# Issuing the odd conditioning-weight transfers of the prelude from GpSimd's queue

## What is computed

```python
cond = silu(c)
for i in range(2):
    mod = einsum('bd,sdk->bsk', cond, ada_w[i]) + ada_b[i]      # ada_w: (2 layers, 2 sub-layers, 2048, 3*2048)
    h = modulate(rmsnorm(x, norm_g[i, 0]), shift_t, scale_t)
    y = pool_mixer(h, ...) if i == 0 else retention(h, ...)
    x = x + gate_t * y
    h = modulate(rmsnorm(x, norm_g[i, 1]), shift_m, scale_m)
    x = x + gate_m * (relu(h @ w1[i]) ** 2 @ w2[i])
return rmsnorm(x, final_g)
```

## Time and profile before

| what | value |
|---|---|
| time, median of 3 runs | 2337.06 us (2336.86 to 2339.1) |
| span of the profiled execution | 2336.1 us |
| own time of the profiled execution | not listed apart from its span |
| TensorE matmul busy | 2251.9 us, 96% |
| VectorE busy | 1681.1 us, 72% |
| ScalarE busy | 1084.2 us, 46% |
| GpSimd busy | 139.9 us, 6% |
| moved by DMA | 664.21 MB, mean 284 GB/s |
| chain that ended last | PE 88%, of it line 701 86% |

### The profile page before, as it was taken

How to read it: one execution, slowest core, us unless ns; L and a number is a source line. 1 busy time by engine, 2 the same in 40 slices (tenths; PEclk the granted TensorE clock), 3 DMA queues, 4 the chain that set the end, 5 groups by cost and what they waited for, 6 DMA issues and landing times.

```text
span 2336.1 us, 28515 instructions
## 1 busy us (share of the span) xinstructions
PE 2251.9 (96%) x10033; PEld 1817.7 (78%) x10033; DVE 1681.1 (72%) x1814; ACT 1084.2 (46%) x1342; POOL 139.9 (6%) x249
## 2 busy tenths in 40 slices
PE   4489999999999999999999999999999999999998
PEld 2147788888888887888888888887888888888887
DVE  4668889788887898777676767677877555555557
ACT  2324554544544545444454444555553453453454
POOL 0000000100100100001000001000100000000000
PEclk9689999999999999999999999999999999999999
DMA  9999989998998977888766887876997776776774
GB/s 400 415 413 393 339 297 328 364 367 277 368 334 292 362 281 231 303 264 275 246 233 215 299 260 244 273 239 202 333 359 248 235 230 195 226 232 191 232 228 152
DMA packets 276674, 664.21 MB, mean 284 GB/s; under 512 B 21768, under 2 KB 22200, under 8 KB 269632
## 3 DMA queue, kind: packets, MB, share of 16 engines
q1 hardware_dynamic: 260320, 611.92, 75.8%
q0 software_dynamic: 15328, 49.87, 6.2%
q10 hardware_dynamic: 896, 0.75, 0.1%
HBM read 638.30 MB, written 24.14 MB: 284 GB/s over the span
## 4 chain that ended last, share of the span: by engine, by line
PE 88%; DMA 2%; DVE 2%; ACT 1%; issue 0%; POOLq 0%; POOL 0%; SPq 0%; DVEq 0%; ACTq 0%
PE acc L701 86%; DMA raw<-in_mlp_w 2%; PE acc L1122 1%; DVE w_lo L1601 1%; PE score_ps L1109 0%; ACT w_hi L1173 0%; DVE ada_acc L1607 0%; PE score_ps L908 0%; PE tb L848 0%; DVE ev L1903 0%; PE tb L983 0%; DVE x L1907 0%; DVE scratch L1773 0%; DVE scratch L1768 0%; PE mod_ps L856 0%
## 5 line engine op out<-in xcount | busy, mean ns | idle before, releaser
L1601 DVE TENSOR_TENSOR w_lo<-raw,w_hi 128x1024 fp32r<-128x1024 f32 x775 | 943.3, 1223 | 558.6 <-ACT w_hi L1173 555.5
L1173 ACT ACTIVATE w_hi<-raw 128x1024 fp32r<-128x1024 f32 x775 | 821.8, 1061 | 1094.8 <-PE acc L701 971.5
L701 PE MATMUL acc<-w_hi,h_lo 128*128 128x512 f32 x1788 | 698.5, 391 | 2.6 <-issue 1.6
L701 PE MATMUL acc<-w_hi,h_hi 128*128 128x512 f32 x1788 | 695.8, 389 | 0.0
L701 PE MATMUL acc<-w_lo,h_hi 128*128 128x512 f32 x1788 | 695.8, 389 | 0.0
L701 PE MATMUL acc<-w_hi,a_lo 128*128 128x512 f32 x1308 | 511.6, 391 | 0.4 <-DVE w_lo L1601 0.4
L701 PE MATMUL acc<-w_lo,a_hi 128*128 128x512 f32 x1308 | 510.3, 390 | 0.0
L701 PE MATMUL acc<-w_hi,a_hi 128*128 128x512 f32 x1308 | 510.0, 390 | 0.0
L701 PEld LDWEIGHTS acc<-w_hi,h_lo 128*128 128x128 f32 x1788 | 335.7, 188 | 75.1 <-issue 4.1
L701 PEld LDWEIGHTS acc<-w_hi,h_hi 128*128 128x128 f32 x1788 | 335.7, 188 | 70.0
L701 PEld LDWEIGHTS acc<-w_lo,h_hi 128*128 128x128 f32 x1788 | 335.8, 188 | 68.5
(11 more groups left out here) (216 smaller groups left out, 912.9 us busy)
## 6 DMA issues: line engine op xcount, KB each, us to landing
raw<-in_mlp_w SPq DMA_DIRECT2D x512, 512.0 KB, 5.1
ada_raw<-in_ada_w SPq DMA_DIRECT2D x248, 512.0 KB, 6.6
raw<-in_ret_w_in SPq DMA_DIRECT2D x192, 512.0 KB, 4.6
ada_early_h<-in_ada_w SPq DMA_DIRECT2D x32, 1024.0 KB, 13.4
raw<-in_ret_w_out SPq DMA_DIRECT2D x64, 512.0 KB, 4.4
ada_raw<-in_ada_w SPq DMA_DIRECT2D x16, 1024.0 KB, 12.5
square_blocks<-ev POOLq DMA_DIRECT2D x112, 128.0 KB, 4.8
ev<-square_blocks POOLq DMA_DIRECT2D x28, 512.0 KB, 6.4
```

Of the source, the lines that this page charges most:

```text
L701: mm = nc.tensor.matmul(acc[pair][t][:], l[:, CK * c + j, tok], w[:, slot, j, :], start=first and j == 0 and i == 0, stop=last and j == CK ...
L1173: nc.scalar.activation(w_hi[:, o % RING], raw[:, o % RING], ACT.Copy).then_inc(hi_ready, 1)
L1601: nc.vector.tensor_tensor(w_lo[:, o % RING], raw[:, o % RING], w_hi[:, o % RING].bitcast(F32), ALU.subtract).then_inc(lo_ready, 1)
```

## The change

The even pieces w0, w2, ... w14 of the three wide segments stay on SP, the odd ones are issued by GpSimd. SP's `load_early` now returns for every slot that isn't a multiple of 4. GpSimd gets `load_odd`, with the same wait for the place's earlier contents. Since a segment's odd pieces are TensorE's and 12 slots hold three of them, GpSimd waits on `ada_pe` alone and SP, in these segments, on `ada_done` alone. The odd pieces signal three new semaphores, `odd_in`, and both readers wait on `wide_in(slot)`. `unsignalled` corrects the counts of segments 3 and 4. GpSimd issues w1 to w9 of segment 0, then the first reciprocal root, then all other odd pieces, then the second root. Places, number and sizes of the transfers stay.

```diff
+        odd_in = [sem(f"odd_wide_piece_in{i}") for i in range(EARLY // 4)]
...
+        def wide_in(slot):
+
+            return odd_in[slot // 4] if slot % 4 else ada_in[slot]
+
         def unsignalled(slot):
 
-            return WIDE_SEGS * SEG // EARLY if slot % 2 else 0
+            return WIDE_SEGS * SEG // EARLY if slot % 4 else 0
...
-                if wide and a % 2:
+                if wide and a % 4:
                     return
...
-                        pe.wait_ge(ada_in[slot], early_loads(seg, a))
+                        pe.wait_ge(wide_in(slot), early_loads(seg, a))
...
-                        dve.wait_ge(ada_in[slot - half], early_loads(seg, a - half))
+                        dve.wait_ge(wide_in(slot - half), early_loads(seg, a - half))
...
+            ada_rows = ada_w.rearrange("i s d (j k) -> (i s) d j k", j=3)
+
+            def load_odd(seg, w):
+
+                g = seg * SEG + 2 * w
+                if g >= EARLY:
+                    if ON_PE[g - EARLY]:
+                        pool.wait_ge(ada_pe, PE_BEFORE[g - EARLY + 1] + 1)
+                    else:
+                        pool.wait_ge(ada_done, DVE_BEFORE[g - EARLY + 1] + 1)
+                slot, to = wide_slot(seg, 2 * w)
+                pool.dma_start(to, ada_rows[0, w * P:(w + 1) * P, seg, :]).then_inc(odd_in[slot // 4], 16)
...
-            for _ in range(2):
-                inverse_root()
+            for w in range(1, 11, 2):
+                load_odd(0, w)
+            inverse_root()
+            for w in range(11, KT, 2):
+                load_odd(0, w)
+            for seg in range(1, WIDE_SEGS):
+                for w in range(1, KT, 2):
+                    load_odd(seg, w)
+            inverse_root()
```

## The result

| | before | after |
|---|---|---|
| median, 12 runs each | 2337.47 us | 2342.59 us |
| lowest to highest | 2336.53 to 2340.18 | 2338.51 to 2345.79 |
| ratio after / before | | 1.0019, interval 1.0011 to 1.0027 |
| span of the profiled execution | 2336.1 us | 2340.1 us |

The ratio is 4.4 us of 2337.5, with an interval from 2.6 to 6.3; the two medians lie 5.1 us apart, which is within it. So the change makes the kernel slightly slower, by about the 0.2% that I had taken for what a measurement can tell. With 12 runs it can be told. Forecast were +3.5 us and 2340.5.

What follows compares the result with a forecast made beforehand. The prediction took the prelude to be bound by DMA transfers of fixed bytes, with TensorE's unchanged stretch after it. Terms 2.48 + 1.0 gave +3.5 us, a forecast of 2340.5 us, range 2334.5 to 2347.5.

Steps and rivals of the forecast that it cites:

- the end of segment 2: Segment 2's last pieces: with queues treated equally, w14 lands last, one piece later; +2.48 us, bounds 0 and 2.48.
- the tail: End of segment 2: after GpSimd issues w15, SP alone feeds the engines with three places; +1.0 us, from 0 to 2.9.
- segments 0 and 1: Ends of these segments: w14 lands with w15, 2.5 us later, but queued transfers cover it; cost 0.
- DMA-bound prelude, fixed bytes: Prelude: DMA engines always busy from 2 to 175 us, bytes unchanged, so DMA time fixed except for rate and empty queues.
- Issue time: Wide pieces: GpSimd gains 24 issues of about 0.58 us, SP loses 24 of 0.33; covered by queued pieces, cost 0.
- Start and root gate: Kernel start: x up to 5 us later, within slack; w11 waits for the first root, bounds 0 and 2.5; both 0.
- The dip: 175 to 185 us, at 359 GB/s: 1.2 us to be won; bounds -1.2 and 0, taken as 0.
- The rate: Wide segments, 119 us of 48 pieces: time per byte alike for both queues; bounds -2.8 and +4.2 us, taken as 0.
- Rival A: Wide pieces: transfers from GpSimd's queue are slower under load; +7.7 us, 2344.8, chance 0.15.
- Rival B: Segment 2's end and 28 to 33 us: DMA engines run dry, on the slower side; +7.9, 2345 us, chance 0.13.
- C: Wide segments: queues keep the order of issue by themselves, nothing changes; 0 to +1, 2337.5 us, chance 0.22.
- D: Prelude: each queue waits for one engine alone, 175 to 185 us fills, best rate; -4.0, 2333 us, chance 0.10.

Runs made afterwards that it cites:

- experiment 2: The change, but only the odd pieces of segments 0 and 1 go by GpSimd's queue, segment 2 as before; 2338.89 against 2337.06 us before, ratio 1.0007.
- Experiment 4: The kernel before, with SP issuing w15 of segment 2 ahead of w14, no second queue; 2341.16 against 2337.06 us before, ratio 1.0019.
- experiment 3: The change, but w15 of segment 2 is issued by SP behind w14; 2339.03 against 2337.06 us before, ratio 1.0010.
- experiment 6: The change, but GpSimd issues all odd pieces of segment 0 ahead of the first reciprocal root; 2342.11 against 2338.05 us before, ratio 1.0017.
- experiment 1: The change, but only segment 2's odd pieces go by GpSimd's queue, segments 0 and 1 as before; 2341.34 against 2337.06 us before, ratio 1.0017.
- experiment 5: The kernel before, with SP issuing w14 of segment 2 ahead of w13, one queue; 2338.40 against 2338.05 us before, ratio 1.0000.
- experiment 7: The change with both the edits of experiment 3 and experiment 6; 2339.09 against 2338.05 us before, ratio 1.0006.

## Why the prediction was right

The change was forecast 3.5 us slower, and it is, by 4.4 (2.6 to 6.3). The step that carries the forecast, +2.48 for the order at the end of segment 2, is what the experiments found: 2.39 us with segment 2 alone, 2.32 with the swap alone. That the sum came so near is in part luck: +1.0 for the tail wasn't there, some 0.5 us from segments 0 and 1 had been put at 0, and 1.0 of the 4.0 us between the profiled executions, or about 2 of the 5.1 between the medians, doesn't arise in the prelude, where I had put all of it. Point by point:

- *DMA-bound prelude, fixed bytes*: held. The share is 1.01 from 2 to 85 us and 1.02 from there to 138. It isn't a fine sign, though: from 35 to 40 us it is 1.01 as well, at 370 GB/s.
- *Issue time*: held. 24 issues of 0.53 us (forecast 0.58), with GpSimd busy 10.55 of the first 83 us. The landing times of the odd pieces are those of a line, as before's:

```profile
L2419 POOL DMA_DIRECT2D ada_early_h<-in_ada_w x16: 527/527/584, 2.9 to 127.7; - x16
...
DMA to landing us min/median/max: 8.6/12.2/19.7
```

- *Start and root gate*, both 0: ScalarE's first square moved from 13.90 to 15.15 us, not by 5, but the root moved by 4.9, from 29.77 to 34.67, past the 33 that I had allowed, and the first fill from 42.86 to 49.09. The slack took up most of it: in experiment 2, where these stand as in the change, the row blocks are 0.53 us late. w11 behind the root did cost some transfers, the 370 GB/s above.
- *The end of segment 2*, +2.48: this is most of it. The row blocks moved by 3.0 us, VectorE's start on w14 by 3.0. Experiment 4 has 2.3 of it without the second queue, experiment 3 takes two thirds of it away with one piece. In one respect the step was too narrow. I had reasoned that two queues share the engines, so that w15 would catch up in the transfer; in the trace w15 is already issued 3.6 us before w14. GpSimd had run ahead because nothing ties the two engines' places together. The equal treatment itself is in the trace too, 1.51 MB by GpSimd's queue and 1.43 by SP's from 131 to 138 us. That agrees with what the Trainium skill says of turns by packet (DMA: Bandwidth & Descriptors, Queues, rings and completion order). How much of GpSimd's lead comes from it isn't shown; the swap on one queue costs nearly the same without it.
- *The tail*, +1.0: not there. Between w12 and w14 the rate was 407 to 412 GB/s. This term failed. SP was alone indeed from about 138 us on, when w15 was nearly all in, but it didn't run short: 397 to 414 GB/s in each us from 139 to 142. I had said that segment 3 can't help, its first pieces standing behind w14. They do, but w14 went out at 131.3 and they from 135.03 on, over 6 us before w14 had landed, and so they were in the line.
- *The dip*, 0 taken from -1.2 to 0: it grew, and moved forward to 155 to 170 us. The loss of the prelude is this one, seen from the DMA side.
- *The rate*, 0 taken from -2.8 to +4.2: 412 against 416 GB/s over 83 us is 0.8 us. It isn't a lower rate of GpSimd's transfers: from 45 to 85 us, where they bring 9.39 of 16.90 MB, the rate is 423 against 421 before. The loss lies ahead of 45 us, at 35 to 40 above all, where experiment 6 mended it by moving an issue. (The upper bound of the term should have been +4.1, 119 x 416 / 402 less 119.)

Rival A fell with experiments 1 and 2. The guess of the Trainium skill (DMA: Bandwidth & Descriptors, Latency and other measured facts) that two DMA engines suffer from GpSimd's rings of descriptors finds no support in them: with 16 pieces by GpSimd the row blocks were 0.5 us late, with 8 others 2.4; no row is split by DMA engine, so it isn't refuted either. Rival B may name a real mechanism, but with a small price: 370 GB/s at 35 to 40 us here, 213 for one us in experiment 6. Its sign, a share under 0.9, is in none of the stretches of 5 us from 5 to 138 us in the change. C held the queues to keep their order by themselves, which the issue times refute. D's gain didn't come: the landing times stayed those of a line. Of the signs, line 856 (144.03) and the chain's DMA (181.81) came where expected. Line 701 taking over at 258 to 260 can't be read from the change, whose chain leaves the DMAs at 194.89; in experiments 1 and 6 it is at 258.48 and 258.96.

What stays open: in experiments 1 to 5 the medians lie 1.3 to 2.2 us further above before's than the takeovers do (4: 4.1 against 1.9; 5: 0.35 against -1.2), in 6 and 7 by 0.6 and -0.4. Experiments 4 and 5 have no second queue, so this rest can't be put down to it alone. Part of it may be the profiled execution of the kernel before, with its span of 2336.1: the median span of the executions beside experiments 1 to 4 was 2335.2, beside 5 to 7 2335.9. The profiled execution of experiment 3 was also the fastest of its eleven, that of 1 the slowest. So with intervals of 0.1% to either side I can't say whether something of the second queue's cost remains in experiments 2, 3 and 7. And the change's runs spread over 7.3 us, before's over 3.7. Why wasn't tried.

## What to carry to other kernels

A wait that ends early is worth something only if the thing waited for then arrives earlier: read the landing time beside the issue wait (13.3 us against 5.1 on an empty queue). Here, where transfers stood in line, a second queue gave nothing. One queue in program order also fixes which transfer comes last; splitting it lets one side run ahead. It is worth looking which piece should be last before a handover: the one with the shorter work behind it brought the row blocks 1.7 us forward in experiment 5, though the total didn't show it. To find out whether a second queue or the order costs, swap two transfers on the single queue: one line, and it gave 2.3 of the 3.0 us at the row blocks here, and the same ratio of times.

## What the runs showed of the hardware that I had not expected

**The clock after a wait.** TensorE's row blocks took 1.93 us in the change for the same 8 instructions that took 1.30 before and 1.04 in experiment 5. Ahead of them TensorE had idled 6.81 us in the change, 2.31 before, and not at all in experiment 5. In experiment 2 they took 1.06 us, with 2.31 us of idleness too. The profile's granted clock tells the levels apart: TensorE has two, 0.50 (1.2 GHz) and 1.00 (2.4 GHz). In the change it is at the lower one from the start of the row blocks:

```profile
144.00:148.60 4.60, 4.57 (x18) 1.43 (x19) 0.76 (x2) 0.00 (x0) 0.00 (x0) 0.50 1.02 405
```

Before, the lower level came too, but only while the row blocks ran (0.86 from 141 to 142 us), and it met the product of w15:

```profile
142.00:145.00 3.00, 3.00 (x15) 1.07 (x8) 0.83 (x2) 0.00 (x0) 0.00 (x0) 0.50 1.03 411
```

So the product of w15 took 1.94 us in the change and 1.95 before, and only the row blocks lost, 0.63 us.

The way from the row blocks to the last load of segment 3 took 37.4 us in the change and 36.6 before (36.55 from 141.02 to 177.57). Over all nine kernels this way goes with the clock of the last column of the table: 34.0 and 34.4 us at 0.95 (experiments 2 and 5), 35.6 at 0.91 (3 and 4), 36.6 at 0.86 (before), 36.8 to 37.6 at 0.82 or 0.83 (the others). Which causes which wasn't tested. None of it reached the takeover: that moved by the same 3.0 us as the row blocks in the change, and in experiment 2, with the shortest way, by 0.8 us less than the row blocks. So here the price of the late piece at the takeover was its lateness and no more.
